# Wider weight blocks in three output projections, and three moved waits, in a two-block hybrid network on one core

## What is computed

```python
def first_block(x, ...):
    mix = hybrid_mixer(h, ...)            # ... return merged @ w_out
    h = layer_norm(DEEPNORM_ALPHA * h + mix, ln1_g, ln1_b)
    ffn = moe(h, ...)                     # 32 experts, top 4
    h = layer_norm(DEEPNORM_ALPHA * h + ffn, ln2_g, ln2_b)

def second_block(x, ...):
    u = rmsnorm(h, norm_mix_w)
    h = h + hybrid_mixer_2(u, ...)        # y_s = gated_group_rmsnorm(y, z, w) @ w_s_out
                                          # merged = sig(gate_a)*y_a + sig(gate_s)*y_s
                                          # return merged @ w_o
    v = rmsnorm(h, norm_ffn_w)
    h = h + conv_gated_mlp(v, ...)        # (silu(conv(h1)) * h3) @ w_down
    return rmsnorm(h, final_norm_w)

def gated_group_rmsnorm(y, z, w):         # 4 groups of 512 features
    yf = (y * silu(z)).reshape(b, s, 4, 512)
    yf = yf * rsqrt(mean(yf * yf, axis=-1) + EPS)
    return yf.reshape(b, s, 2048) * w
```

## Time and profile before

| | us |
|---|---|
| median of 3 runs | 1875.41 (1872.4 to 1879.01) |
| profiled execution, its own time | 1878.23 |
| its span | 1876.4 |
| PE busy | 1757.6 (94%) |
| DVE busy | 703.1 (37%) |
| ACT busy | 570.7 (30%) |
| mean granted TensorE clock | 0.966 |

### The profile page before, as it was taken

How to read it: one execution, slowest core, us unless ns; L and a number is a source line. 1 busy time by engine, 2 the same in 40 slices (tenths; PEclk the granted TensorE clock), 3 DMA queues, 4 the chain that set the end, 5 groups by cost and what they waited for, 6 DMA issues and landing times. The chain is left out here.

```text
span 1876.4 us, 26867 instructions
## 1 busy us (share of the span) xinstructions
PE 1757.6 (94%) x11209; PEld 1214.6 (65%) x11209; DVE 703.1 (37%) x1191; ACT 570.7 (30%) x774; POOL 65.6 (3%) x50
## 2 busy tenths in 40 slices
PE   6989969999999999999999999949999998979997
PEld 6989854434444344344343443449999888979997
DVE  3668641211111122112111111153695554557643
ACT  4733510101111111011111110144564676356432
POOL 2003000000000000000000000000100111000000
PEclk9999968999999999999999999979999999989999
DMA  8344466999999999999999999924554432635542
GB/s 256 123 133 135 153 248 255 431 429 430 430 429 431 430 430 430 429 431 430 430 430 430 431 430 430 388 71 143 173 180 155 135 113 93 200 106 187 182 155 77
DMA packets 159862, 534.97 MB, mean 285 GB/s; under 512 B 5507, under 2 KB 123395, under 8 KB 127040
## 3 DMA queue, kind: packets, MB, share of 16 engines
q1 hardware_dynamic: 158560, 531.06, 71.9%
q0 software_dynamic: 1248, 3.14, 0.6%
HBM read 533.13 MB, written 1.05 MB: 285 GB/s over the span
## 5 line engine op out<-in xcount | busy, mean ns | idle before, releaser
L1098 PE MATMUL bank<-expert_weights,x_gathered 128*64 128x512 f32 x1536 | 338.5, 595 | 2.6 <-DMA expert_weights<-in_expert_w_up_dram 2.6
L106 DVE TENSOR_TENSOR m_w_lo<-raw_weights,m_w_hi 128x2048 fp32r<-128x2048 f32 (+1 forms) x120 | 278.6, 2325 | 162.5 <-ACT m_w_hi L102 161.3
L102 ACT ACTIVATE m_w_hi<-raw_weights 128x2048 fp32r<-128x2048 f32 (+1 forms) x120 | 227.2, 1894 | 134.6 <-PE bank L120 107.5
L1098 PEld LDWEIGHTS bank<-expert_weights,x_gathered 128*64 128x64 f32 x1536 | 106.7, 137 | 211.5 <-issue 200.9
L1114 PE MATMUL bank<-expert_weights_late,activations 128*64 128x512 f32 x1024 | 226.8, 595 | 0.0
L118 PE MATMUL bank<-u_hi,m_w_hi 128*128 128x256 f32 x704 | 202.6, 288 | 3.4 <-DVE u_lo L1429 3.4
L119 PE MATMUL bank<-u_lo,m_w_hi 128*128 128x256 f32 x704 | 200.7, 285 | 0.0
L120 PE MATMUL bank<-u_hi,m_w_lo 128*128 128x256 f32 x704 | 200.7, 285 | 0.0
L1005 DVE COPY step_cols<-expert_slots 128x2 f32 (+1 forms) x33 | 5.6, 169 | 445.3 <-PE bank L1081 445.3
L1032 DVE TENSOR_TENSOR pre_act<-bank,bias_now 128x512 f32<-128x512 f32 x64 | 44.0, 688 | 315.3 <-PE bank L1105 315.3
L1114 PEld LDWEIGHTS bank<-expert_weights_late,activations 128*64 128x64 f32 x1024 | 70.7, 137 | 130.1 <-issue 127.9
(11 more groups left out here) (376 smaller groups left out, 2669.8 us busy)
## 6 DMA issues: line engine op xcount, KB each, us to landing
expert_weights<-in_expert_w_up_dram SPq DMA_DIRECT2D x96, 2048.0 KB, 19.3
expert_weights_late<-in_expert_w_down_dram SPq DMA_DIRECT2D x64, 2048.0 KB, 17.6
raw_weights<-in_expert_w_up_dram SPq DMA_DIRECT2D x32, 2048.0 KB, 19.4
raw_weights<-in_w_in_dram SPq DMA_DIRECT2D x62, 1024.0 KB, 5.3
raw_weights<-in_w_up_dram SPq DMA_DIRECT2D x22, 1024.0 KB, 5.1
raw_weights<-in_w_s_out_dram SPq DMA_DIRECT2D x8, 1024.0 KB, 5.0
raw_weights<-in_w_down_dram SPq DMA_DIRECT2D x8, 1024.0 KB, 4.9
raw_weights<-in_w_out_dram SPq DMA_DIRECT2D x4, 1024.0 KB, 5.2
```

The source lines that it names most:

```text
L102: act.activation(self.s.w_hi[:, s, 0:size], self.s.raw[:, s, 0:size], ACT.Copy).then_inc(self.hi_done, 1)
L106: dve.tensor_tensor(self.s.w_lo[:, s, 0:size], self.s.raw[:, s, 0:size], self.s.w_hi[:, s, 0:size].bitcast(FP32), ALU.subtract).then_inc(s ...
L1098: m = pe.matmul(U[b][rows[half], :], lhsT=xg[:, 2 * u + a, :], rhs=w[:, a, 512 * c:512 * c + 512], start=(first and a == 0), stop=(last an ...
```

## The change

- The three output projections take units of 4 row tiles by 512 columns (the last down unit of a column block: 2 row tiles). A new `rows_out` has each token tile write its own bank with 512 moving columns and signals the first token tile's bank on its own (`out_first`); DVE adds each token tile's 512 columns by itself. The first projection waits for two banks before its first unit, not one.
- In mixer2 PE takes the mean squares of groups 0, 1, 2 in n = 35, 38, 42, between that unit's products and `scan_out`; of group 3 between units 45 and 46. ACT squares in the same places as before and makes the reciprocal root one unit later; `group_hi` and `group_lo` follow one unit later. After the scan ACT squares group 3 first, and rounds unit 47 before it asks for the mean square.
- The down projection has twelve units: two blocks of 512 columns by 4, 4, 4, 4, 4, 2 row tiles. Each unit of the first block waits only for the feature pairs that it reads.

```diff
+def rows_out(pe, banks, w, kt, x_of, first, last, tile_done, unit_done):
+    for t in range(TT):
+        c = slice(t * P, (t + 1) * P)
+        for k in range(kt):
+            m = product3(pe, banks[t][:, :], (x_of(0, k)[:, c], x_of(1, k)[:, c]), (w[0][:, k, :], w[1][:, k, :]),
+                         first and k == 0, last and k == kt - 1)
+        if last and t == 0:
+            m.then_inc(tile_done, 1)
+    m.then_inc(unit_done, 1)
```

PE in mixer1 (`w_o` in mixer2 alike, in banks 4 to 7 and without a wait for a bank):

```diff
                 for u in range(NO_UNITS):
-                    n, b = NW + NB_UNITS + u, NW + 8 + u
+                    n, c, kh = NW + NB_UNITS + u, u // 2, u % 2
                     pe.wait_ge(st.lo_done, n + 1)
-                    wait_bank(pe, b)
-                    tokens_out(pe, s.bank[b % 2], st.w(n % 3, KD, COLS), None, KD, merged_part).then_inc(st.gemm_done, 1)
+                    if u == 0:
+                        wait_bank(pe, NW + 8)
+                        wait_bank(pe, NW + 9)
+                    rows_out(pe, s.bank[2 * c:2 * c + 2], st.w(n % 3, 4, 512), 4, lambda part, k: merged_part(part, 4 * kh + k),
+                             kh == 0, kh == 1, out_first, st.gemm_done)
```

ACT in mixer2, where the root becomes a function of its own:

```diff
+                def group_rstd(g):
                     act.wait_ge(ms_mm, g + 1)
...
                         if n == at:
                             group_squares(g)
-                        if n == at + 1 and g < 2:
+                        if n == at + 1:
+                            group_rstd(g)
+                        if n == at + 2 and g < 2:
                             group_hi(g)
+                group_squares(3)
                 group_hi(2)
-                group_squares(3)
+                split_hi(act, 47)
+                group_rstd(3)
                 group_hi(3)
-                for n in range(44, 56):
+                for n in range(45, 56):
```

PE in mixer2:

```diff
                     unit(n, ya if n < 32 else u)
-                    scan_out(n - 28)
-                    for g, at in ((0, 34), (1, 37), (2, 41)):
+                    for g, at in ((0, 35), (1, 38), (2, 42)):
                         if n == at:
                             mean_squares(g)
+                    scan_out(n - 28)
                 pe.wait_ge(y_done, 8)
                 for n in range(44, 48):
-                    if n == 45:
+                    if n == 46:
                         mean_squares(3)
```

And `ffn`:

```diff
-    UP_UNITS, DOWN_K = 2 * D_FF // COLS, (8, 8, 6)
-    N_UNITS = UP_UNITS + 4 * len(DOWN_K)
+    UP_UNITS, DOWN_K = 2 * D_FF // COLS, (4, 4, 4, 4, 4, 2)
+    N_UNITS = UP_UNITS + 2 * len(DOWN_K)
...
-                pe.wait_ge(evac_sem[(UP_UNITS - 1) % 3], (UP_UNITS - 1) // 3 + 1)
+                def wait_features(kk):
+                    for f in range(4 * kk, 4 * kk + DOWN_K[kk], 2):
+                        u = UP_UNITS // 2 + f // 2
+                        pe.wait_ge(evac_sem[u % 3], u // 3 + 1)
...
                     pe.wait_ge(st.lo_done, n + 1)
+                    if c == 0:
+                        wait_features(kk)
```

More of the change, by code:

```diff
@@ L241, in mixer1 @@
         bias_loaded, bias_mm, bias_ready = sem("bias_loaded"), sem("bias_mm"), sem("bias_ready")
+        out_first, out_added = sem("out_first"), sem("out_added")
         var_ready, ln_rstd, h_ready, ht_mm, ht_out, lg_mm = (sem(n) for n in (
@@ L284, in _ @@
                         n += 1
[L285 to L288, removed]
+                for c in range(2):
+                    for kh in range(2):
+                        w = A["w_out"][0].rearrange("(k p) n -> p k n", p=P)
+                        st.load(sp, n // 3, n % 3, w[:, 4 * kh:4 * kh + 4, 512 * c:512 * c + 512], 4, 512)
+                        n += 1
                 sp.wait_ge(hgr_out, 4)
@@ L641, in _ @@
                     split_lo(dve, NW + u)
[L643 to L650, removed]
+                for c in range(2):
+                    for t in range(TT):
+                        if t == 0:
+                            dve.wait_ge(out_first, c + 1)
+                        else:
+                            dve.wait_ge(st.gemm_done, NW + 8 + 2 * c + 2)
+                        hc = s.h[:, t, 512 * c:512 * c + 512]
+                        dve.scalar_tensor_tensor(out=hc, in0=hc, scalar=DEEPNORM_ALPHA, in1=s.bank[2 * c + t][:, :],
+                                                 op0=ALU.mult, op1=ALU.add).then_inc(out_added, 1)
+                dve.wait_ge(out_added, 4)
                 layer_norm(dve, own, s.h, stats, mv, var_ready, ln_rstd, ln_g, ln_b, ln_loaded, 32, h_ready)
@@ L1213, in mixer2 @@
         S_OUT = [(c, kh) for kh in range(2) for c in range(4)]
+        O_OUT = [(c, kh) for c in range(2) for kh in range(2)]
         N_UNITS = 56
         bank_seq = [(n, n % 3) for n in range(44)]
-        bank_seq += [(48 + c, c) for c in range(4)] + [(52 + c, c % 3) for c in range(4)]
+        bank_seq += [(48 + c, c) for c in range(4)]
         bank_of, use_of = {}, {}
@@ L1248, in unit @@
                         return A["w_s_out_2"][0].rearrange("(a k p) n -> a p k n", p=P, k=KD)[kh, :, :, COLS * cb:COLS * cb + COLS]
-                    return A["w_o_2"][0].rearrange("(k p) n -> p k n", p=P)[:, :, COLS * (n - 52):COLS * (n - 51)]
-                for n in range(3, N_UNITS):
+                    c, kh = O_OUT[n - 52]
+                    return A["w_o_2"][0].rearrange("(k p) n -> p k n", p=P)[:, 4 * kh:4 * kh + 4, 512 * c:512 * c + 512]
+                for n in range(3, 52):
                     st.load(sp, n // 3, n % 3, unit(n), KD, COLS)
+                for n in range(52, N_UNITS):
+                    st.load(sp, n // 3, n % 3, unit(n), 4, 512)
                 for i in (2, 0, 1):
@@ L1547, in _ @@
                     split_lo(dve, n + 3)
-                    for g, at in ((0, 36), (1, 39)):
+                    for g, at in ((0, 37), (1, 40)):
                         if n == at:
@@ L1552, in _ @@
                 group_lo(2)
+                split_lo(dve, 47)
                 group_lo(3)
-                for n in range(44, 52):
+                for n in range(45, 52):
                     if n >= 48:
@@ L1567, in _ @@
                     split_lo(dve, n + 3)
[L1568 to L1572, removed]
+                for c in range(2):
+                    for t in range(TT):
+                        if t == 0:
+                            dve.wait_ge(out_first, c + 1)
+                        else:
+                            dve.wait_ge(st.gemm_done, 52 + 2 * c + 2)
+                        hc = s.h[:, t, 512 * c:512 * c + 512]
+                        dve.tensor_tensor(hc, hc, s.bank[4 + 2 * c + t][:, :], ALU.add).then_inc(h_done, 1)
             @block.tensor
@@ L1583, in _, with gemm @@
                 pe.wait_ge(ut_lo, KD)
-                def gemm(q, i, bank, x, tokens=False, first=True, last=True, used=None):
+                def gemm(q, i, bank, x, first=True, last=True, used=None):
                     pe.wait_ge(st.lo_done, q * 3 + i + 1)
@@ L1589, in gemm @@
                         pe.wait_ge(evac_sem[bank], used)
[L1590 to L1599, removed]
+                    features_out(pe, s.bank[bank], st.w(i, KD, COLS), x, 0, KD, first, last).then_inc(st.gemm_done, 1)
                 def unit(n, x, **kw):
@@ L1769, in _ @@
                         c, k = DOWN[n - UP_UNITS]
-                        st.load(sp, n // 3, n % 3, w_down[:, 8 * k:8 * k + DOWN_K[k], COLS * c:COLS * c + COLS], DOWN_K[k], COLS)
+                        st.load(sp, n // 3, n % 3, w_down[:, 4 * k:4 * k + DOWN_K[k], 512 * c:512 * c + 512], DOWN_K[k], 512)
                 for t in range(TT):
@@ L1862, in _ @@
                     if k == len(DOWN_K) - 1:
-                        hc = s.h[:, :, COLS * c:COLS * c + COLS]
-                        dve.wait_ge(st.gemm_done, n + 1)
-                        dve.tensor_tensor(hc, hc, s.bank[4 + c][:, :].rearrange("p (a n) -> p a n", a=2), ALU.add).then_inc(evac_sem[3], 1)
+                        for t in range(TT):
+                            if t == 0:
+                                dve.wait_ge(out_first, c + 1)
+                            else:
+                                dve.wait_ge(st.gemm_done, n + 1)
+                            hc = s.h[:, t, 512 * c:512 * c + 512]
+                            dve.tensor_tensor(hc, hc, s.bank[4 + 2 * c + t][:, :], ALU.add).then_inc(evac_sem[3], 1)
                 dve.wait_ge(evac_sem[3], 4)
@@ L1901, in _ @@
                     pe.wait_ge(st.lo_done, n + 1)
-                    w = st.w(n % 3, DOWN_K[kk], COLS)
-                    for t in range(TT):
-                        for k in range(DOWN_K[kk]):
-                            f, tok = 8 * kk + k, slice(P * t, P * t + P)
-                            m = product3(pe, s.bank[4 + c][:, COLS * t:COLS * t + COLS], (p_hi[:, f, tok], p_lo[:, f, tok]),
-                                         (w[0][:, k, :], w[1][:, k, :]), kk + t + k == 0, kk == len(DOWN_K) - 1 and k == DOWN_K[kk] - 1, True)
-                    m.then_inc(st.gemm_done, 1)
```

(4 more changed lines are left out.)

21 lines of the change are left out of this document (14 added, 7 removed).

## The result

The median is 1853.35 us (1852.69 to 1855.82, four runs), beside 1875.28 of the kernel before on the same chip: ratio 0.9875, interval 0.9849 to 0.9900, so 21.9 us less by the medians and 23.4 by the ratio (18.8 to 28.3). The forecast was 1847 in a range from 1841 to 1856. The sign and the places were right, the gain was 28.8 us on paper and 21.9 to 23.4 on the chip.

The account below looks back on a forecast made before the run. Outside the DMA-heavy expert stretch, PE's work and waits in mixer1, mixer2 and ffn were taken as the bound. 10.9 + 9.2 + 3.3 + 0.7 + 4.7 = 28.8 us off 1878.2, less 2.8 for the median, gave 1847; range 1841 to 1856.

Parts of the forecast that it names:

- Term 1: Three output projections: 912 matmuls of 256 columns become 456 of 512, each saving 0.024 us, 10.9 us in all.
- a maximum, not a sum: Projection matmuls: something taking 0.12 us whatever the clock, most likely the next tile's load, hides behind 512 columns; 0.216 us each.
- The first rival: Projections: the load shows at any width, 0.227 us per 512-column matmul; gain 24.0 us, time 1851, chance 0.12.
- Term 2: Second mixer's group norm: PE's four waits for squares, 10.3 us, go; new waits cost 1.1 us; gain 9.2 us.
- The margin of minus 0.2 us per step: Scan: the chain to `scan_out` takes 9.3 us where PE wants it after 9.1, so PE waits 0.2 us in two steps.
- Term 3: Scan: without the waits for squares, full clock returns behind groups 0 and 3; gain 3.3 us, bounds 0 and 3.3.
- Term 4: Second mixer's projection: the wait for the last `ya_lo` goes, 0.7 us; first mixer's `x_lo` wait is exchanged for a bank, 0.
- Term 5: Down projection's start: the 3.0 us wait for `p_lo` goes and 1.7 us of clock returns; gain 4.7 us.
- The scan's chain: Scan: PE waits at `scan_out` instead and the clock falls as before; norm and clock gains shrink to about 3; 1856, chance 0.08.
- the void wait: Down projection: its new wait does nothing, because its first units' weights are late next; time 1851, chance 0.05.
- two passes: Projections, slower case: 512 fp32r columns need two passes per 256, 0.86 us per matmul, 283 us more; time 2129, chance 0.02.
- 0.131 us per matmul: Projections: 512-column matmuls come much closer than one column per cycle allows; sum 67.6 us, time 1808, chance 0.02.

## Why the prediction was right, and where it was wrong

- **Term 1 failed, in size.** It took 0.216 us per 512-column matmul from the fp32 rows and reasoned that the 13 ns are a load longer than 256 fast and shorter than 256 slow columns. The matmuls start 0.227 us apart, and the term is 456 x (0.240 - 0.2267) = 6.1 us, not 10.9. The step that failed is "a maximum, not a sum". The 13 ns are a sum at full clock, at 384 and 512 columns too. At half clock there are none, and that is why the rows pointed the wrong way; fp32 was the wrong neighbour, since it lacks them. The maximum is there as well, as a floor of 0.110 us, but it is not where the 13 ns come from. The first rival had the right number: it gave 24.0 us, and the four stretches that the change touches gave 24.8. Its reason, a load that doesn't overlap, fell with the 0.110 us of 128 columns, and taken as written the rule would have asked for far more than 13 ns at 256 columns.
- **Term 2 held.** The four waits for squares went (10.3 us); the new ones are 1.5 us, not 1.1: 8.8 instead of 9.2. The margin of minus 0.2 us per step was minus 0.3. Group 3 brought no wait, as taken.
- **Term 3 held.** Full clock in both stretches. Terms 2 and 3 together gave 13.1 us, forecast 12.5. But that the waits took 3.3 us of clock belongs to the one execution that was profiled: with the columns alone the same four waits had half clock behind one of them, not two.
- **Term 4 held for the second mixer**: its projection gave 2.4 us, 0.9 of it the wait, as its 0.7 us of idle time were 0.9 between starts. In the first mixer 0 was taken for the exchange of `x_lo` against the second bank. The gap before the projection grew by 1.14 us and the wait for `x_lo` (0.9 between starts) went, so it cost some 0.2 us; moving the banks took the whole 1.14 away.
- **Term 5 held.** The gap went from 3.25 to 0.12 us (3.1, forecast 3.0), and of the 5.1 us by which the projection itself is shorter 3.5 are the wider matmuls (264 x 0.0133), 1.6 the clock (forecast 1.7).
- **The other rivals.** The scan's chain showed only in those 1.5 us of waits at `scan_out`; the void wait, two passes and 0.131 us per matmul did not show. The Trainium skill's spacing for 512 columns (TensorE: Matmul & The Clock Gate, Back-to-back issue gap) is not seen in fp32r here. Two sums are off: the slower rival's time is 1875.4 + 283 - 17.9 = 2140 us, not 2129, which counts term 1's gain although that rival has none; and the lower end of the range comes to 1842, not 1841.

So the touched stretches fell 4.0 us short of the forecast: 4.8 by term 1 and 0.2 at the first projection, against 0.6 in the scan and 0.4 at the second projection that they gave over their forecasts. Besides, the start of the program is 4.2 us longer, the two untouched stretches are 2.6 us shorter by the clock, and the remaining code is 0.7 us longer. These 2.3 us are not the change's; another execution may have them otherwise.

## What to carry to other kernels

Let an engine ask for another engine's result one unit of its own work later: here that was 13 us of the 22, as four waits of under 3 us each also took the clock behind two of them in the profiled execution. Price a wider instruction by rows of the same data type and at the clock at which it will run. Do the part of a norm that needs only half of the columns while the other half is still multiplied, and group activations by function: with 9.5 us this was worth more than the wider blocks.

## What the runs showed of the hardware that was not expected

- A matmul in fp32r has about 13 ns on top of its cycles at full clock, whatever its width from 256 up (0.120, 0.175 and 0.227 us for 256, 384 and 512), and with half the tile loaded (0.230) or the bank changed (0.227); none at half clock (0.213 and 0.427 us for 256 and 512), and some 2.5 ns per instruction in fp32.
- Under that lies a floor of 0.110 us, most likely the load of 128 columns. It is gone (0.060 us) behind a 128-column matmul that itself followed one of 384 columns.
- A wait of the same length isn't always followed by half clock. PE waits 2.1 us for `gates` before the first `hg` matmul in both kernels, at 210.97 us before and 215.20 after. The 5 us behind it, the first row of before, the second of after (length, busy and count, clock, DMA share, GB/s):

```profile
211.00:216.00 5.00, 5.00 (x29) 0.66 0.81 261
```

```profile
215.00:220.00 5.00, 4.80 (x40) 1.00 0.84 236
```

The branches on `hg` last 12.9 us with the half clock and 11.5 without it. Of the twelve profiles of this study, all with the same wait at this place, seven have it and five don't, kernels of the same code up to there among both. What decides it stays open; no run here was made to tell.
